# Retrieval queries held in on-chip space beside attention buffers and layer-norm weights, y computed in place, stages one step later

## What is computed

```python
def _layer(x, ...):
    m = _mixer(x, ...)                        # RG-LRU, short conv, attention to 256 memory tokens
    x = _layernorm(DEEPNORM_ALPHA * x + m, lp['ln1_g'], lp['ln1_b'])
    f = _peer(x, lp['peer_wq'], lp['peer_keys'], lp['peer_u'], lp['peer_v'])
    x = _layernorm(DEEPNORM_ALPHA * x + f, lp['ln2_g'], lp['ln2_b'])

def block(xb):                                # _peer, 128 tokens at a time
    qb = jnp.einsum('td,de->te', xb, wq).reshape(PEER_BLOCK, PEER_HEADS, 2, PEER_DK // 2)
    sk = jnp.einsum('thpd,hpkd->thpk', qb, keys)
    v1, i1 = lax.top_k(sk[:, :, 0], PEER_TOPK)
    v2, i2 = lax.top_k(sk[:, :, 1], PEER_TOPK)
    cand = (v1[..., :, None] + v2[..., None, :]).reshape(...)
    top_s, ci = lax.top_k(cand, PEER_TOPK)
    e = i1[ci // 16] * N_KEYS + i2[ci % 16]
    g = jax.nn.softmax(top_s, axis=-1)
    act = jax.nn.gelu(jnp.einsum('td,thkd->thk', xb, u_tab[e]))
    return jnp.einsum('thk,thkd->td', g * act, v_tab[e])
```

## Time and profile before

| what | value |
|---|---|
| median of 3 runs | 3215.14 us (3214.41 to 3221.25) |
| the profiled execution's own time | 3219.03 us |
| its span, first to last instruction | 3217.2 us |
| DMA traffic | 1261.33 MB, 1140.92 MB of it gathers |
| PE, DVE, ACT, POOL busy | 78%, 67%, 43%, 38% |
| mean granted TensorE clock | 0.84 |

### The profile page before, as it was taken

One profiled execution on the slowest core, in us unless ns is written; L12 is line 12 of the kernel. 1 busy time (PEld: TensorE's weight loads), 2 busy tenths in 40 slices (PEclk: granted clock), 3 DMA queues, 4 the chain that ended last, 5 costly groups with the idle time before them and its releaser, 6 DMA issues.

```text
span 3217.2 us, 35895 instructions
## 1 busy us (share of the span) xinstructions
PE 2513.9 (78%) x10052; PEld 720.9 (22%) x10052; DVE 2151.4 (67%) x4930; ACT 1397.2 (43%) x4023; POOL 1218.8 (38%) x1092
## 2 busy tenths in 40 slices
PE   8989978788877997688877878877666667666676
PEld 4543422222111332223321113311111111100010
DVE  3575678878666476878767686656676666664554
ACT  3334446556434334465544353334443344443343
POOL 0023434344334443344434434434334444433342
PEclk9989989999897998999889979966776776676776
DMA  5349999999999999999999999999999999999997
GB/s 211 120 190 415 420 417 411 371 392 400 420 420 416 420 420 418 393 396 414 419 420 411 420 412 420 401 399 421 421 414 420 421 416 404 421 421 418 405 418 316
DMA packets 199767, 1261.33 MB, mean 392 GB/s; under 512 B 24208, under 2 KB 27536, under 8 KB 59664
## 3 DMA queue, kind: packets, MB, share of 16 engines
q0 software_dynamic: 156672, 1140.92, 86.1%
q1 hardware_dynamic: 42752, 117.60, 9.7%
q10 hardware_dynamic: 144, 0.52, 0.1%
HBM read 1241.30 MB, written 17.66 MB: 391 GB/s over the span
## 4 chain that ended last, share of the span: by engine, by line
issue 53%; POOL 35%; PE 6%; DMA 4%; DVE 1%; POOLq 1%; ACT 0%; SPq 0%; DVEq 0%; ACTq 0%
POOL arena L684 35%; DMA arena<-in_uv,idxT 3%; PE ps L711 2%; PE ps L963 1%; POOLq L676 1%; PE ps L841 0%; PE ps L731 0%; DMA arena<-in_w_in 0%; PE ps L861 0%; PE ps L947 0%; PE ps L882 0%; DVE arena L1576 0%; PE ps L912 0%; DMA arena<-in_xT 0%; SPq L536 0%
## 5 line engine op out<-in xcount | busy, mean ns | idle before, releaser
L684 POOL DMA_INDIRECT arena<-in_uv,idxT x1088 | 1218.6, 1120 | 1969.7 <-PE ps L963 1703.3
L963 PE MATMUL ps<-arena,wset 128*32 128x512 f32 x4352 | 1412.5, 750 | 647.1 <-ACT wset L1170 571.2
L1576 DVE CUSTOM_DVE_ANT_0 arena<-arena 128x1024 f32<-128x1024 f32 x1088 | 1328.6, 1224 | 841.0 <-DMA arena<-in_uv,idxT 793.7
L1161 ACT ACTIVATE gel<-acts 128x1 f32<-128x1 f32 x1088 | 219.6, 202 | 1400.0 <-DVE acts L1576 1394.1
L963 PEld LDWEIGHTS ps<-arena,wset 128*32 128x32 f32 x4352 | 176.2, 119 | 1593.0 <-ACT wset L1170 1346.6
L1170 ACT ACTIVATE wset<-arena,wt 128x32 f32<-128x32 f32 x1088 | 349.5, 321 | 36.1
L1165 ACT ACTIVATE wt<-gel,gT 128x1 f32<-128x1 f32 x1088 | 320.5, 295 | 102.8 <-ACT gel L1161 3.0
L711 PE MATMUL ps<-arena 128*128 128x384 f32 (+1 forms) x768 | 310.7, 526 | 13.2 <-DMA arena<-in_xT 6.8
L882 PE MATMUL ps<-arena 128*128 128x384 f32 (+3 forms) x896 | 288.6, 452 | 10.2 <-DMA arena<-in_wq 8.4
L947 PE MATMUL ps<-arena 32*128 32x512 f32 x640 | 222.8, 778 | 0.0
L882 PEld LDWEIGHTS ps<-arena 128*128 128x128 f32 x896 | 147.3, 191 | 204.3 <-issue 163.2
(11 more groups left out here) (173 smaller groups left out, 1513.7 us busy)
## 6 DMA issues: line engine op xcount, KB each, us to landing
arena<-in_wq SPq DMA_DIRECT2D x56, 512.0 KB
arena<-in_w_in SPq DMA_DIRECT2D x47, 512.0 KB
arena<-in_uv,idxT POOLq DMA_INDIRECT x1088
arena<-in_w_outs SPq DMA_DIRECT2D x24, 512.0 KB, 9.3
arena<-scratch_q SPq DMA_DIRECT2D x30, 256.0 KB
arena<-in_x_tok SPq DMA_DIRECT2D x9, 512.0 KB, 12.8
scratch_x<-arena SPq DMA_DIRECT2D x9, 512.0 KB
scratch_q<-arena SPq DMA_DIRECT2D x8, 512.0 KB
```

The source lines that it names most:

```text
L684: pool.indirect_dma_start(out=ring[n % RING], out_offset=None, in_=A["uv"], in_offset=bass.IndirectOffsetOnAxis(ap=idxT[t % 2][:, col:col ...
L963: last = mm(ps[r0:r0 + 32, hf * HALF:(hf + 1) * HALF], wset[n % SETS][:, :], v[:, hf * HALF:(hf + 1) * HALF], start=first, stop=final)
L1161: A_(gel[:, n % COLS:n % COLS + 1], acts[:, n % COLS:n % COLS + 1], ACT.Gelu).then_inc(gelus, 1)
L1576: V.tensor_tensor_reduce(out=ring[n % RING][:, 0:D], in0=ring[n % RING][:, 0:D], in1=xrep[g % 2], scale=1.0, scalar=0.0, op0=ALU.mult, op1 ...
```

## The change

Four things are changed.

1. **Queries stay on chip.** `q_all` is one area of 3 x 4 x 512 columns: one place for each tile of a block (t % 3) and quarter k. ACT's `we` and `wa` write there for all tiles of the block at once, PE's `keyscores` reads there. The tensor `q` in DRAM, its stores (`sq`), `load_q`, `stg`, `qTb` and all their waits are gone. For tile 0, quarters 0 and 1 lie in the recurrence's temporaries, after a wait for the short convolution of block 0 (`sh`, which is earlier in the order). `wa` writes three tiles with one instruction, where it wrote two.
2. **What shares that space.** The attention buffers `prob` and `probT` are the places of tile 0 (t % 3 = 0), and the first layer norm's weights `ln1` those of tile 1. Queries overwrite `ln1`, so blocks 1 and 2 load it again (1 MB each) at step BASE + 150, after a wait for the last key scores of the tile that lies there. `ex` of an attention's first round and `we` of each quarter wait for the key scores of the tile whose place they overwrite.
3. **y in place.** `finish(t)` writes into `x1b[t % 2]`; `yout` is gone. The x1 of tile t is now loaded 20 steps after tile t - 2 ends and after a wait for that tile's y store, instead of 5 steps after and upon `res_done`. Two of the eight tiles of block 0's output weights move to other space.
4. **Steps.** In blocks 1 and 2 `ra` and `re`, and `ex`, `nz`, `at`, `tc` stand one step later (`nz` one and a half), as does the recurrence group's norm (`nm`, `no`). The pieces of `route` begin two steps into a window instead of one, and `select` and the copies of indices and gates follow one step later.

```diff
     put("sp", o - 6, b, "xT")
+    put("sp", o + 150, b, "ln")
...
-        put("dve", x + 17, b, "ra", c)
+        put("dve", x + 18, b, "ra", c)
         put("dve", x + 20, b, "rc", c)
         put("act", x + 23, b, "sd", c)
-        put("dve", x + 24, b, "re", c)
+        put("dve", x + 25, b, "re", c)
...
-        put("act", x + 1, b, "ex", r)
-        put("dve", x + 1.5, b, "nz", r)
-        put("pe", x + 4, b, "at", r)
-        put("act", x + 5, b, "tc", r)
+        put("act", x + 2, b, "ex", r)
+        put("dve", x + 3, b, "nz", r)
+        put("pe", x + 5, b, "at", r)
+        put("act", x + 6, b, "tc", r)
...
-        if side % 4 == 3:
-            put("sp", x + each * (side + 1) + 1, b, "sq", side // 4)
...
-    stg = [temps[:, i * 3 * 512:(i + 1) * 3 * 512] for i in range(2)]
-    prob = [a.take(2 * NM) for _ in range(2)]
-    probT = [a.take(2 * NM) for _ in range(2)]
+    queries = a.take(3 * 4 * 4 * P)
+    q_all = queries.rearrange("p (t k f) -> p t k f", t=3, k=4)
+    prob = [q_all[:, 0, i, :] for i in range(2)]
+    probT = [q_all[:, 0, 2 + i, :] for i in range(2)]
...
+    ln1 = q_all[:, 1, :, :].rearrange("p k f -> p (k f)").rearrange("p (i n) -> p i n", i=2)
+    ln2 = a.take(2 * D).rearrange("p (i n) -> p i n", i=2)
     keysT = a.take(SIDES * NK)
-    qTb = [a.take(4 * P) for _ in range(2)]
...
-    yout = a.take(D)
...
+    def q_of(t, k):
+
+        if t == 0 and k < 2:
+            return temps[:, k * 4 * P:(k + 1) * 4 * P]
+        return q_all[:, t % 3, k, :]
...
-        return 1 + i // per(u)
+        return 2 + i // per(u)
...
-        def load_q(u):
-
-            t, k = UNIT[u]
-            b = min(t // 3, 2)
-            sp.wait_ge(k_mm, u - 1)
-            for kk in ([k] if t < TILES else [k, k + 2]):
-                sp.wait_ge(st_q[kk % 2], q_stores(b, kk))
-            load(ld_q[u % 2], qTb[u % 2], O["q"][t, :, k, :])
...
-                sp.dma_start(O["q"][t0:t0 + n_, :, k, :].rearrange("t p f -> p t f"),
-                             s_[:, 0:n_ * 512].rearrange("p (t f) -> p t f", t=n_)).then_inc(st_q[k % 2], 16)
...
+            elif name == "ln":
+                sp.wait_ge(k_mm, scored(3 * b - 2, 3))
+                load("ln", ln1, A["ln"][0:2].partition_broadcast(P))
...
-        x1_at = {max(TILE_END[t - 2] + 5, s1_at[t] + 3): t for t in range(2, TILES + 1)}
+        x1_at = {max(TILE_END[t - 2] + 20, s1_at[t] + 3): t for t in range(2, TILES + 1)}
...
             if n in x1_at:
-                sp.wait_ge(res_done, x1_at[n] - 1)
+                sp.wait_ge(st_y, 48 * (x1_at[n] - 1))
...
-            if u < 4:
-                after(pe, "act", 0, "w0" if u < 2 else "wa", 4 * u + 3)
-            else:
-                pe.wait_ge(ld_q[u % 2], 16 * (u // 2 - 1))
+            b = min(t // 3, 2)
+            for kk in ([k] if t < TILES else [k, k + 2]):
+                after(pe, "act", b, "we" if b or (t and kk < 2) else "w0" if kk < 2 else "wa", 4 * kk + 3)
...
-            for k in range(4):
-                if q_order(b - 1, k) >= 2:
-                    act.wait_ge(st_q[k % 2], q_stores(b - 1, k))
+            if b == 1:
+                act.wait_ge(k_mm, scored(0, 1))
...
+                if arg == 0 and b:
+                    act.wait_ge(k_mm, scored(3 * b - 3, 3))
...
-                if q_order(b, k) >= 2:
-                    act.wait_ge(st_q[k % 2], q_stores(b, (k + 2) % 4))
...
-                if name == "wa":
-                    act.wait_ge(k_mm, k - 1)
-                    A_(qTb[k % 2][:, si * P:(si + 1) * P], bk[:, 0:P], ACT.Copy)
-                    bk = bk[:, P:]
+                if b and si == 0:
+                    act.wait_ge(k_mm, scored(3 * b - 1, k))
...
+                ins = A_(q_all[:, t0:t1, k, si * P:(si + 1) * P],
+                         bk[:, 0:(t1 - t0) * P].rearrange("p (t n) -> p t n", t=t1 - t0), ACT.Copy)
...
-            dve.wait_ge(st_y, 48 * t)
-            did(V.scalar_tensor_tensor(yout, x1b[t % 2], ALPHA, ybank, ALU.mult, ALU.add))
+            yout = x1b[t % 2]
+            did(V.scalar_tensor_tensor(yout, yout, ALPHA, ybank, ALU.mult, ALU.add))
...
-                for _ in range(per(u)):
-                    next(pieces, None)
+                if at >= 2:
+                    for _ in range(per(u)):
+                        next(pieces, None)
```

More of the change, by code:

```diff
@@ L165, in plan_later_block @@
         x = o + 150
-    for g, at, no in ((G_LRU, 115.5, 119), (G_MEM, 118 if b == 1 else 142, 124 if b == 1 else 145), (G_SC, 133, 136)):
+    for g, at, no in ((G_LRU, 116.5, 120), (G_MEM, 118 if b == 1 else 142, 124 if b == 1 else 145), (G_SC, 133, 136)):
         for k in GROUPS[g][1]:
@@ L493, in nbank, with scored @@
         return 0 if b == 0 else MB[2] if g == G_MEM else MB[1]
[L495 to L502, removed]
+    def scored(t, k):
+        return UNIT.index((t, k)) + 1
+    def q_of(t, k):
+        if t == 0 and k < 2:
+            return temps[:, k * 4 * P:(k + 1) * 4 * P]
+        return q_all[:, t % 3, k, :]
     def last_query(b):
@@ L632, in _ @@
             mix(v)
-        load("ln", ln_v[:, 0:2, :], A["ln"][0:2].partition_broadcast(P))
+        load("ln", ln1, A["ln"][0:2].partition_broadcast(P))
         for i in range(KD):
@@ L653, in _ @@
                 load_x1(1)
-                load("ln2", ln_v[:, 2:4, :], A["ln"][2:4].partition_broadcast(P))
+                load("ln2", ln2, A["ln"][2:4].partition_broadcast(P))
             t = SLOT[n][0]
             if n in x1_at:
-                sp.wait_ge(res_done, x1_at[n] - 1)
+                sp.wait_ge(st_y, 48 * (x1_at[n] - 1))
                 load_x1(x1_at[n])
@@ L907, in keyscores @@
                 pe.wait_ge(gT_ready, u)
-            qs = qTb[u % 2]
             for si in range(4):
@@ L911, in keyscores @@
                 if t < TILES:
-                    last = mm(kbank[:, si * NK:(si + 1) * NK], qs[:, si * P:(si + 1) * P], keysT[:, a_:a_ + NK],
+                    last = mm(kbank[:, si * NK:(si + 1) * NK], q_of(t, k)[:, si * P:(si + 1) * P], keysT[:, a_:a_ + NK],
                               start=True, stop=True)
@@ L917, in keyscores @@
                         last = mm(kbank[half * NS:(half + 1) * NS, si * NK:(si + 1) * NK],
-                                  qs[:, si * P + half * NS:si * P + (half + 1) * NS], keysT[:, b_:b_ + NK],
+                                  q_of(t, k + 2 * half)[:, si * NS:(si + 1) * NS], keysT[:, b_:b_ + NK],
                                   start=True, stop=True)
@@ L1099, in run @@
             elif name == "w0":
-                u_, si = arg // 4, arg % 4
+                k, si = arg // 4, arg % 4
+                if arg == 0:
+                    after(act, "dve", b, "sh", CS - 1)
                 after(act, "pe", b, "w0", arg)
-                ins = A_(qTb[u_ % 2][:, si * P:(si + 1) * P], bank[MB[arg % 3]][:, 0:P], ACT.Copy)
+                ins = A_(q_of(0, k)[:, si * P:(si + 1) * P], bank[MB[arg % 3]][:, 0:P], ACT.Copy)
             elif name in ("wa", "we"):
@@ L1435, in run @@
                 if hf == 0:
[L1436 removed]
+                    dve.wait_ge(ld["ln"], 16 * (b + 1))
                     after(dve, "act", b, "dv", ti)
                     link(V.reciprocal(mv1[:, 3:4], mv1[:, 2:3]))
[L1439 to L1440 removed]
+                link(V.scalar_tensor_tensor(z_, z_, mv1[:, 0:1], ln1[:, 0, c_], ALU.subtract, ALU.mult))
+                did(V.scalar_tensor_tensor(z_, z_, mv1[:, 3:4], ln1[:, 1, c_], ALU.mult, ALU.add))
                 finished()
@@ L1664 @@
         O[name] = nc.dram_tensor("out_" + name, shape, F32, kind="ExternalOutput").ap()
-    for name, shape in (("x1", ((TILES + 1) * P, D)), ("q", (TILES + 1, P, 4, 4 * P))):
-        O[name] = nc.dram_tensor("scratch_" + name, shape, F32).ap()
+    O["x1"] = nc.dram_tensor("scratch_x1", ((TILES + 1) * P, D), F32).ap()
     build(nc, A, O)
```

41 lines of the change are left out of this document (11 added, 30 removed).

## The result

The changed kernel takes **3180.3 us** (median of 4 runs, 3176.8 to 3181.2) against 3215.9 (4 runs, 3214.4 to 3221.3). The ratio is 0.9882, 95% interval 0.9870 to 0.9893: 38 us less, with an interval of 34 to 42. The forecast was 3181, 34 us less, with a range of 3167 to 3198. Measured again beside other kernels it was 3178.0, ratio 0.9880 (0.9864 to 0.9897).

What follows compares the result with a forecast made beforehand. The prediction took the DMA engines to bound the kernel from about 230 us on. Removed traffic 37.6, less 7.6 lost, plus 4.0 from steps gave 34.0 us less: 3215.1 to 3181 us, range 3167 to 3198.

Steps and rivals of the forecast that it cites:

- The bound: From about 230 us on the DMA engines bind; a byte SP no longer moves brings the next gather forward.
- The marks named ahead: SP's queue about 104 MB, 8.5 or 8.6% of span; lead unchanged; query-stretch slots 2.8 to 2.9 us; 0.7 us per vanished load.
- The price of the removed traffic: Query loads and stores, 15.73 MB at 2.75 us per MB, 43.3 us; less new layer-norm loads, 37.6 us elapsed.
- What is lost where DMA is not alone the bound: 2.9 us lost at 280 to 360 us, where PE is full, and 4.7 us in starved stretches: together 7.6 us.
- The steps: Later steps shorten DVE's waits where DMA starves, in blocks 1 and 2: 4 us gained, between -8 and 13.2.
- Costed at nothing: ACT's dropped copies, layer-norm loads, key-score waits, SP's y-store wait at 12.8 us landing and y in place: 0 us.
- a sign of a misjudged cover: PE or SP standing for y stores or layer-norm weights would show that a cover was misjudged.
- The sum: Whole kernel: 37.6 - 7.6 + 4.0 = 34.0 us less, from 3215.1 to 3181 us.
- Compute did not take over: Rival: PE binds wherever queries are made, 15 us lost, gain 22.6 down to 14.6, 3192 to 3200 us; chance 0.20.
- The shift frees: Rival: later steps free the starved stretches, 13.2 us instead of 4, 47 us gained, 3168 us; chance 0.15.
- Hidden anyway: Rival: query loads and stores were already overlapped, so removing them gains nothing: 3216 us; chance 0.04.
- The clock: Rival: TensorE meets its lower clock in the query stretches, 44 us more against 34 gained, 3225 us; chance 0.04.

Runs made afterwards that it cites:

- e4: The changed kernel plus 16 idle stores and 30 idle loads, query traffic nobody waits for (15.73 MB): 3215.8 us, ratio 0.9992 to the kernel before.
- e6: The changed kernel plus the 16 idle stores alone (7.86 MB): 3200.5 us, ratio 0.9938 to the kernel before.
- e7: The changed kernel plus 15.73 MB of idle stores in 2 KB rows, four stores at each of 15 places: 3210.4 us, ratio 0.9982 to the kernel before.
- e8: The changed kernel plus 15.73 MB of idle stores in 8 KB rows, one store at each of 15 places: 3212.5 us, ratio 0.9985 to the kernel before.
- e5: The changed kernel plus the 30 idle loads of 256 KB alone (7.86 MB): 3199.1 us, ratio 0.9943 to the kernel before.
- e2: The changed kernel with all step numbers of before put back: 3183.6 us, ratio 0.9897 to the kernel before.
- e1: The kernel before with only the step numbers of the change, queries still through DRAM: 3209.1 us, ratio 0.9972.
- e3: The kernel before with only y computed in place and the later x1 load: 3214.9 us, ratio 0.9993.

## Why the prediction was right, step by step

- **The bound** was right: the same GB/s, fewer bytes, and traffic that nobody waits for costs its full time (e4 to e6). The marks named ahead came true: 103.96 MB (forecast about 104), 8.5% of the span, an unchanged lead, shorter slots in block 1's query stretch. One was too high: from slot 720 on seven loads are gone, and the changed kernel gains 3.7 us on the kernel before there, 0.5 us each and not 0.7.
- **The price of the removed traffic** was set too high. The step that took 2.75 us per MB because the rows are 2 KB, and came to 37.6 us net of the two new loads, is refuted by e7 and e8: 2 KB rows cost no more than 8 KB rows, 2.1 us of elapsed time per MB in both, and 2.3 to 2.5 in e4 to e6. Priced by the rate of a full stretch, which stands in the row GB/s, the term is 13.64 MB / 420 GB/s = 32.5 us. The packets' own time is longer for the short rows, as the prediction read, but the kernel does not become longer by it. The Trainium skill's rule on packet overhead (DMA: Bandwidth & Descriptors, "Why small descriptors are slow (HBM only)") would have given an estimate of 39.5 us for the removed traffic instead of 43.3: nearer, but also a price by row length, of which no run here shows a part in the elapsed time.
- **What is lost where DMA is not alone the bound**, 7.6 us, was too large. The 2.9 us taken off for a full PE at 280 to 360 us come back behind that stretch: at slot 96 e6 has lost 4.6 of 5.0 us. For the 4.7 us in starved stretches: e5 costs 20 us of a full price of 18.7, so no loss shows, within the 6 us that its ratio's interval and the changed kernel's leave, while e7 up to slot 240 would allow one. e2, the traffic's share alone, is 33 us (28 to 38), as 32.5 without any loss.
- **The steps** were forecast to give 4 us and gave 5 (changed kernel against e2) to 9 (e1). The mechanism was right for the mixer's steps, in the stretch at 720 to 760 us that the prediction named; in block 2's, at 1330 to 1410 us, nothing was gained. It was wrong for the routing: that wait moved to `finish`.
- **Costed at nothing**: y in place and the later x1 load (e3), in spite of SP's four waits for the y store, which the prediction put at none for a landing of 12.8 us. SP standing for y stores was named as a sign of a misjudged cover; the cover was short, and it cost nothing that can be told.
- **The sum**: 37.6 - 7.6 + 4.0 was forecast; the runs say 32.5 - 0 + 5 to 9. The first two errors cancel to within 3 us, and the third makes the rest. That the forecast came within 1 us of the median is in part luck: by the ratio it was 4 us short.
- **The rivals.** Compute did not take over: PE set the pace of the issues in a part of 280 to 360 us, but the stores' price was paid behind it, and in block 1's query stretch the traffic cost its full bytes (e4). "The shift frees" wanted 13 us; the shift gave 5 to 9, and the stretch at 560 to 680 us stayed starved (0.96). "Hidden anyway" falls by e4. The clock stayed where it was (0.92 in both kernels in steps 288 to 368).

## What to carry to other kernels

When all DMA engines are busy through a stretch, price a transfer by its bytes at the GB/s that the stretch shows, not by the durations of its own packets; as long as such a stretch lasts, it costs this even if nobody waits for it, so a round trip through DRAM costs twice its bytes even if it is perfectly prefetched. To find out what a transfer costs, put the same bytes back with nobody waiting: it takes one run, and separates traffic from coupling. Read its price not in the window where it is issued but some tens of slots later, slot against slot, and put a second profile of the unchanged kernel beside it: a count of gathers in a fixed window moved by one with nothing changed. Here a wait was worth removing only where DMA starved. Look also at which engine is late there: if another instruction waits for the same engine one step on, the wait changes its name and nothing is gained.

## What the runs showed of the hardware

- Stores of 2 KB rows and of 8 KB rows cost the same elapsed time beside a stream of 8 KB gathers (32 and 33 us for 15.73 MB, within 4), although their packets' summed time differs by some 6 us.
- With PE busy for all of 303 to 362 us, the issues of slots 36 to 56 kept the same distance from the changed kernel's within 0.01 us when stores were added (e6), and the price of the stores came out later: 4.6 of 5.0 us at slot 96, in one profile of each.
- One core's 16 DMA engines moved 419 GB/s in all from 1030 to 1260 us, gathers and SP's traffic together.
